# The last down projection with 16 of its 44 weight chunks as seven block products

## The reference

```
f = rms_norm_2(h, ffn_norm_g)
h = h + (silu(f @ ffn_w1) * (f @ ffn_w3)) @ ffn_w2        # ffn_w2: 5632 x 2048
h = h + (p @ pl_w_up) * sigmoid(h @ pl_w_gate)            # pl_w_gate: 2048 x 2048
return rms_norm_2(h, final_norm_g)
```

## Time and profile before

| | us |
|---|---|
| median of 3 runs | 2418.42 (2418.24 to 2418.65) |
| profiled execution: span from the first to the last instruction | 2417.2 |
| profiled execution: its own time | the profile gives the span alone; the median is 1.2 above it |
| TensorE busy in it | 2404.8 (99%), 10956 matmuls |
| VectorE busy | 1389.7 (57%) |
| ScalarE busy | 1170.4 (48%) |
| GpSimd busy | 127.4 (5%) |
| DMA queue of SP, share of 16 engines | 68.0% |

### The profile page before, as it was taken

The page is one execution under the profiler, slowest core; times in us unless marked ns, Lnnn a source line. Parts: engine busy times, 40 slices in busy tenths (PEclk is TensorE's granted clock), DMA queues, the critical chain, the costliest instruction groups (busy, mean ns, idle before and its releaser), DMA issues.

```text
span 2417.2 us, 27743 instructions
## 1 busy us (share of the span) xinstructions
PE 2404.8 (99%) x10956; PEld 2000.9 (83%) x10956; DVE 1389.7 (57%) x1192; ACT 1170.4 (48%) x1110; POOL 127.4 (5%) x138
## 2 busy tenths in 40 slices
PE   9999999999999999999999999999999999999998
PEld 8888888888888888888888888888888888888886
DVE  6877645656666666544666474664545445444446
ACT  5554554656656556333455464454343433433335
POOL 5000000001111011000000000000010100100000
PEclk9999999999999999999999999999999999999999
DMA  7566556587777778755698855776766767666663
GB/s 257 187 205 204 167 179 199 179 301 237 234 243 252 235 235 253 276 205 193 202 299 279 254 174 175 231 245 211 230 211 214 221 208 226 231 225 213 213 229 123
DMA packets 276834, 535.16 MB, mean 221 GB/s; under 512 B 12634, under 2 KB 47376, under 8 KB 275856
## 3 DMA queue, kind: packets, MB, share of 16 engines
q1 hardware_dynamic: 276304, 533.21, 68.0%
q10 hardware_dynamic: 448, 0.79, 0.1%
HBM read 495.15 MB, written 39.59 MB: 221 GB/s over the span
## 4 chain that ended last, share of the span: by engine, by line
PE 99%; ACT 1%; DVE 0%; DMA 0%; issue 0%; DVEq 0%; SPq 0%; ACTq 0%
PE ps L1462 31%; PE ps L1464 31%; PE ps L1463 31%; PE ps L1455 2%; PE ps L1456 1%; PE ps L1700 1%; PE ps L1438 0%; PE ps L1715 0%; DMA h<-in_x_dram 0%; ACT w_hi L819 0%; PE ps L1840 0%; PE ps L1684 0%; PE ps L1721 0%; PE ps L1751 0%; DVE w_lo L1898 0%; ACT g_work L984 0%
## 5 line engine op out<-in xcount | busy, mean ns | idle before, releaser
L1898 DVE TENSOR_TENSOR w_lo<-raw,w_hi 128x2048 fp32r<-128x2048 f32 x424 | 980.5, 2312 | 986.4 <-ACT w_hi L819 986.1
L819 ACT ACTIVATE w_hi<-raw 128x2048 fp32r<-128x2048 f32 x424 | 812.8, 1917 | 1207.7 <-PE ps L1464 1168.5
L1462 PE MATMUL ps<-w_hi,xa 128*128 128x512 f32 x1856 | 723.6, 390 | 0.0
L1464 PE MATMUL ps<-w_hi,xa 128*128 128x512 f32 x1856 | 722.2, 389 | 0.0
L1463 PE MATMUL ps<-w_lo,xa 128*128 128x512 f32 x1856 | 722.1, 389 | 0.0
L1462 PE MATMUL ps<-w_hi,g 128*128 128x512 f32 x1408 | 549.2, 390 | 0.0
L1464 PE MATMUL ps<-w_hi,g 128*128 128x512 f32 x1408 | 547.9, 389 | 0.0
L1463 PE MATMUL ps<-w_lo,g 128*128 128x512 f32 x1408 | 547.8, 389 | 0.0
L1464 PEld LDWEIGHTS ps<-w_hi,xa 128*128 128x128 f32 x1856 | 348.4, 188 | 72.7
L1462 PEld LDWEIGHTS ps<-w_hi,xa 128*128 128x128 f32 x1856 | 348.4, 188 | 72.4 <-DVE w_lo L1905 0.2
L1463 PEld LDWEIGHTS ps<-w_lo,xa 128*128 128x128 f32 x1856 | 348.4, 188 | 71.8
(11 more groups left out here) (315 smaller groups left out, 997.6 us busy)
## 6 DMA issues: line engine op xcount, KB each, us to landing
raw<-in_ffn_w_dram SPq DMA_DIRECT2D x132, 1024.0 KB, 5.2
raw<-in_w_in_dram SPq DMA_DIRECT2D x94, 1024.0 KB, 5.2
raw<-in_w_up_dram SPq DMA_DIRECT2D x88, 1024.0 KB, 5.9
raw<-in_w_down_dram SPq DMA_DIRECT2D x44, 1024.0 KB, 5.4
raw<-in_w_out_dram SPq DMA_DIRECT2D x32, 1024.0 KB, 5.1
raw<-in_w_pg_dram SPq DMA_DIRECT2D x16, 1024.0 KB, 7.2
raw<-in_pl_w_gate_dram SPq DMA_DIRECT2D x16, 1024.0 KB, 6.0
up_turned_rows<-h SPq DMA_DIRECT2D x22, 512.0 KB, 3.0
```

What stands on the lines that cost most here:

```text
L819: A(w_hi[j % SPLIT][:, :], raw[s][:, :], ACT.Copy).then_inc(sem("w_hi_ready"), 1)
L1462: mm(o, high, hi, start=begin, stop=False)
L1464: return mm(o, low, hi, start=False, stop=end)
L1898: V.tensor_tensor(w_lo[j % SPLIT][:, :], raw[j % RAW][:, :], w_hi[j % SPLIT][:, :].bitcast(F32), ALU.subtract).then_inc(sem("w_lo_ready"), 1)
```

## The change

In each of `down2` and `down2b` a chunk now holds two k-tiles of 128 rows and all 1024 columns, not four k-tiles and 512 columns; all four banks are filled from chunk 0 to chunk 21. For the 28 ordinary chunks `eight_products` issues 24 matmuls, first those of banks 0 and 1, then those of banks 2 and 3. For chunks 3, 5, ... 17 of each stage `seven_products` issues 21: the 2x2 block product (two token halves, two k-tiles, two column halves) is done with seven block products, not eight. That takes sums of weight blocks and sums of activation blocks.

The weight sums: GpSimd makes the first two (`early_sums`), VectorE the third in place in `raw` and the fourth (`late_sums`); `high` of that chunk waits for the third; ScalarE rounds the three sums that are not in `raw` (`sums_high`), VectorE takes their low parts (`low_sums`). The activation sums ("forms"): during `glu` GpSimd makes four of 128x128 for each of eight iterations (`form_sums`, `form_lows`), ScalarE rounds them, SP stores them in DRAM, and in `down2` and `down2b` SP reads them back, 512 KB for each of the 16 chunks (`take_forms`, behind the load of the chunk two later). The products go to banks 4 to 7 as well; VectorE merges them after chunk 17.

The quads of `h` are turned elsewhere: quads 0 and 1 at positions 3 and 7 of `down2b` (SP's transfers at 8, 9, 12 and 13), quads 2 and 3 at position 21 of it (SP's transfers in `pg2`). The return of the 2 MB embedding and the gain row moves from `down2` and the start of `pg2` to the second iteration of `pg2`. Some semaphores of earlier stages are merged, with the same waits.

```diff
+SEVEN = {"down2": (3, 5, 7, 9, 11, 13, 15, 17), "down2b": (3, 5, 7, 9, 11, 13, 15, 17)}
+SEVEN_BEFORE = {"down2": 0, "down2b": 8}
+FORM_TILES = range(1, 9)
...
+            def paired(ph, w, c0, at):
+
+                for j in range(plan[ph]["body"]):
+                    if j in at:
+                        at[j]()
+                    load(ph, 0, j, weight(w, 2 * j, 2, c0, 1024))
+                    if j - 2 in SEVEN[ph]:
+                        take_forms(ph, j - 2)
+
+            def put_forms(e):
+
+                first = (e - 1) * 1024
+                sp.wait_ge(sem("forms_low"), e)
+                sp.dma_start(forms_dram[:, first:first + 1024] if isinstance(e, int) else forms_dram[:, bass.ds(first, 1024)],
+                             forms[:, :].bitcast(F32)).then_inc(sem("forms_stored"), 16)
+
+            def take_forms(ph, c):
+
+                n, first = SEVEN[ph].index(c), (c // 2 - 1) * 1024
+                sp.wait_ge(sem("forms_stored"), 16 * (c // 2))
+                sp.wait_ge(sem("chunks_multiplied"), chunk_no(ph, 0, c - 4) + 1 if n >= 2 else plan[ph]["chunk"])
+                sp.dma_start(form_factors[ph][n % 2].bitcast(F32), forms_dram[:, first:first + 1024]).then_inc(sem(f"forms_landed{n % 2}"), 16)
...
-                if ph == "pg1":
+                if ph == "pg1" or (ph, q) == ("pg2", 3):
...
+            def glu_fifth(i):
+
+                if isinstance(i, int) and i == 0:
+                    take_h_blocks("glu", 2)
+                elif not isinstance(i, int) or i >= 3:
+                    put_forms(i - 2)
+
+            columns("glu", [(t["ffn_w1_2"][0], 0), (t["ffn_w3_2"][0], 0)], 512, peel=3,
+                    at={4: at_step(0, lambda: put_h_blocks("glu", 2)), 5: glu_fifth,
                         6: lambda i: put_h_blocks("glu", 3) if isinstance(i, int) and i == 0 else put_blocks(i),
                         7: lambda i: take_h_blocks("glu", 3) if isinstance(i, int) and i == 0 else take_blocks(i)})
             w = t["ffn_w2_2"][0]
-            columns("down2", [(w, 0), (w, 512)], 1024, kts=FT,
-                    at={6: lambda i: put_blocks(plan["glu"]["iters"]), 7: lambda i: take_blocks(plan["glu"]["iters"]),
-                        8: take_second,
-                        16: lambda i: put_h_blocks("pg2", 0), 17: lambda i: take_h_blocks("pg2", 0)})
-            columns("down2b", [(w, 1024), (w, 1536)], 1024, kts=FT,
-                    at={5: lambda i: put_h_blocks("pg2", 1), 6: lambda i: take_h_blocks("pg2", 1),
-                        16: lambda i: put_h_blocks("pg2", 2), 17: lambda i: take_h_blocks("pg2", 2)})
+            paired("down2", w, 0,
+                   at={6: lambda: put_blocks(plan["glu"]["iters"]), 7: lambda: take_blocks(plan["glu"]["iters"])})
+            paired("down2b", w, 1024,
+                   at={8: lambda: put_h_blocks("pg2", 0), 9: lambda: take_h_blocks("pg2", 0),
+                       12: lambda: put_h_blocks("pg2", 1), 13: lambda: take_h_blocks("pg2", 1)})
             columns("pg2", [(t["pl_w_gate_2"][0], 0), (t["pl_w_gate_2"][0], 512)], 1024, peel=2,
-                    at={5: at_step(0, lambda: put_h_blocks("pg2", 3)),
-                        6: both(at_step(0, lambda: take_h_blocks("pg2", 3)), load_final_row)})
+                    at={0: at_step(1, lambda: take_h_blocks("pg2", 3)), 2: at_step(1, take_second),
+                        6: at_step(0, lambda: put_h_blocks("pg2", 2)),
+                        7: at_step(0, lambda: (take_h_blocks("pg2", 2), put_h_blocks("pg2", 3))), 5: at_step(1, lambda: load_final_row(0))})
...
+            def form_sums(e):
+
+                if not (isinstance(e, int) and e == FORM_TILES[0]):
+                    pool.wait_ge(sem("forms_stored"), (e - 1) * 16)
+                of = lambda k, a: staged_tile(staged, k)[:, a]
+                s1, s2, s3, s4 = [forms_work[:, 512 + P * n:512 + P * (n + 1)].rearrange("p (i r) -> p i r", r=32) for n in range(4)]
+                pool.tensor_tensor(s3, of(2, 0), of(2, 1), ALU.subtract)
+                pool.tensor_tensor(s1, of(2, 1), of(3, 1), ALU.add).then_inc(sem("forms_summed"), 1)
+                pool.wait_ge(sem("forms_summed"), e * 3 - 2)
+                pool.tensor_tensor(s2, s1, of(2, 0), ALU.subtract).then_inc(sem("forms_summed"), 1)
+                pool.wait_ge(sem("forms_summed"), e * 3 - 1)
+                pool.tensor_tensor(s4, of(3, 0), s2, ALU.subtract).then_inc(sem("forms_summed"), 1)
+
+            def form_lows(e):
+
+                pool.wait_ge(sem("forms_high"), e)
+                pool.tensor_tensor(forms[:, 512:1024], forms_work[:, 512:1024], forms[:, 0:512].bitcast(F32), ALU.subtract)\
+                    .then_inc(sem("forms_low"), 1)
+
             def glu_lows(i):
+                formed = not isinstance(i, int) or i in FORM_TILES
+                if isinstance(i, int) and i == plan["glu"]["iters"] - 1:
+                    early_sums("down2", SEVEN["down2"][0])
                 pool.wait_ge(sem("glu_high"), i + 1)
+                if formed:
+                    form_sums(i)
                 for a in range(2):
                     last = pool.tensor_tensor(in_blocks(g[:, bass.ds(i * 4, 4), S + a * P:S + (a + 1) * P]), staged_half(staged, a),
                                               in_blocks(g[:, bass.ds(i * 4, 4), a * P:(a + 1) * P].bitcast(F32)), ALU.subtract)
                 last.then_inc(sem("glu_low"), 1)
+                if formed:
+                    form_lows(i)
+
+            def early_sums(ph, c):
+
+                no = seven_no(ph, c)
+                pool.wait_ge(sem(f"raw_landed{c % RAW}"), landed_count(ph, c))
+                n = SEVEN[ph].index(c)
+                pool.wait_ge(sem("chunks_multiplied"), chunk_no(ph, 0, c - 4) + 1 if n >= 2 else plan[ph]["chunk"])
+                blocks = raw[c % RAW][:, :].rearrange("p (k b n) -> p b k n", k=2, b=2)
+                pool.tensor_tensor(sums[no % 2][:, 0:1024].rearrange("p (k n) -> p k n", k=2), blocks[:, 1],
+                                raw[c % RAW][:, 0:1024].rearrange("p (k n) -> p k n", k=2), ALU.subtract).then_inc(sem("early_sums"), 1)
...
-            iterations(pool, "glu", glu_lows)
+            iterations(pool, "glu", glu_lows, peel=2, tail=2)
+            for ph in SEVEN:
+                for c in SEVEN[ph][ph == "down2":]:
+                    early_sums(ph, c)
...
+                seven = ph in SEVEN and i == 0 and j in SEVEN[ph]
+                if seven:
+                    act.wait_ge(sem("sums"), 2 * seven_no(ph, j) + 1)
                 A(w_hi[j % SPLIT][:, :], raw[s][:, :], ACT.Copy).then_inc(sem("w_hi_ready"), 1)
+                if seven:
+                    act.wait_ge(sem("sums"), 2 * seven_no(ph, j) + 2)
+                    A(sums_high[ph], sums[seven_no(ph, j) % 2], ACT.Copy).then_inc(sem("sums_high"), 1)
...
+                SEVEN["down2"][-1]: lambda i: copy_first_product("down2")})
             stream("down2b", unroll=True, at={
-                3: lambda i: staged_high("pg2", 1),
-                14: lambda i: staged_high("pg2", 2)})
+                6: lambda i: staged_high("pg2", 0),
+                10: lambda i: staged_high("pg2", 1),
...
+                1: steps({0: lambda: staged_high("pg2", 2)}),
...
+            def three(b, high, low, hi, lo, begin, end):
+
+                mm(bank(b), high, hi, start=begin, stop=False)
+                mm(bank(b), high, lo, start=False, stop=False)
+                return mm(bank(b), low, hi, start=False, stop=end)
+
+            def eight_products(ph, j, hi, lo):
+
+                for gr in range(2):
+                    if j == 0:
+                        group_free(ph, 0, gr)
+                    for a in range(2):
+                        for k in range(2):
+                            x = g[:, 2 * j + k, :]
+                            c = slice((2 * k + gr) * 512, (2 * k + gr + 1) * 512)
+                            last = three(2 * gr + a, x[:, a * P:(a + 1) * P], x[:, S + a * P:S + (a + 1) * P], hi[:, c], lo[:, c],
+                                         j == 0 and k == 0, j == plan[ph]["body"] - 1 and k == 1)
+                        if j == plan[ph]["body"] - 1 and gr != a:
+                            last.then_inc(sem("half_multiplied"), 1)
+                return last
+
+            def seven_products(ph, j, hi, lo):
+
+                no, n = seven_no(ph, j), SEVEN[ph].index(j)
+                begin, end = n == 0, j == SEVEN[ph][-1]
+                slot_ = form_factors[ph][n % 2]
+                early, late = g[:, 2 * j, :], g[:, 2 * j + 1, :]
+                block_ = lambda w, b: w[:, 512 * b:512 * (b + 1)]
+                form = lambda m: (slot_[:, P * m:P * (m + 1)], slot_[:, 512 + P * m:512 + P * (m + 1)])
+                if begin and no:
+                    pe.wait_ge(sem("products_read"), 1)
+                three(4, early[:, 0:P], early[:, S:S + P], block_(hi, 0), block_(lo, 0), begin, end)
```

(90 more changed lines are left out.)

161 lines of the change are left out of this document (94 added, 67 removed).

## The result

| us | before | after |
|---|---|---|
| median (range) | 2418.33 (2417.97 to 2418.65), 4 runs | 2448.98 (2445.93 to 2450.93), 4 runs |
| profiled execution: its time / its span | span 2417.2 | 2445.93 / 2444.2 |
| last matmul starts | 2407.61 | 2434.59 |
| TensorE busy, matmuls | 2404.8, 10956 | 2405.0, 10908 |

The account below looks back on a forecast made before the run. The prediction took TensorE, 99% of the chain, to bound the kernel. Seven terms added 35.4 us and removed matmuls took 10.9 off: +24.5 on the span of 2417.2, 2441.7, with 1.2 for the median 2443 us, range 2427 to 2454.

Parts of the forecast that it names:

- (c): Rival: the clock falls in all four long waits, costing 12 in place of 4.1, plus longer waits: 2453 us; chance 0.13.
- step 3: `down2b`, chunks 7 and 11: forms land late, queued behind the turned quads' store and reads; 4.7 us each, 9.5 together.
- step 4: `pg2` (start P), chunks 2 and 4: turn of quad 3 and reads of quad 2 hold up weights; 2.7 and 2.9, 5.6 us.
- step 7: Granted clock falls in three long waits, and matmuls run at half rate for a while afterwards; 4.1 us (0 to 12).
- step 6: `glu`: GpSimd's activation sums make its second low meet a `w_lo` in eight iterations; 1.0 us (0 to 2.5).
- step 1: `down2`, chunk 0: banks 2 and 3 are wanted while the gate product stands behind `w_lo` of chunk 1; 3.6 us.
- step 2: `down2`, chunk 5: GpSimd's weight sum stands behind `glu_lows`, and its next sum blocks VectorE's third; 6.5 us.
- step 5: Pairs in `down2`, `down2b`: GpSimd's sums block VectorE, late loads, second turn and `add_pair` add delays; 5.1 us (1.5 to 8).
- (b): Rival: GpSimd and VectorE do not block each other for these operand shapes; 2431 us; chance 0.12.
- (a): Rival: the slack holds, TensorE stays busy and 10.9 go; faster, 2407.5 or up to 2412 us; chance 0.05.

Follow-up runs that it names:

- e12: e9 with the last block product of each of the 16 chunks of 21 issued twice, so 24 matmuls in every chunk: 2422.58 us.
- e9: Against the kernel after: gate product first, nothing on GpSimd in `down2` and `down2b`, quads, last low half and `glu_high` moved behind urgent work: 2411.93 us.
- e1: Kernel after, but in the last `glu` iteration VectorE does the gate product before `w_lo` of chunk 1 of `down2`: 2443.26 us.
- e2: Kernel after, but GpSimd makes the weight sum of chunk 5 of `down2` before the last `glu_lows`: 2441.34 us.
- e7: Kernel after, but GpSimd's sum of chunk 7 of `down2` waits until VectorE has made the third sum of chunk 5: 2448.87 us.
- e10: Kernel after, but VectorE makes `early_sums` in front of `w_lo` of the chunk before, not GpSimd: 2435.71 us.
- e3: Kernel after, but in `down2b` SP issues the forms of chunks 7 and 11 ahead of the store of the turned quad: 2445.76 us.
- e4: Kernel after, but quad 3 has its own buffer and DRAM rows, and SP reads quad 2 right behind its store: 2440.44 us.
- e11: e9 with the first two weight sums of each chunk of 21 back on GpSimd, 16 instructions: 2416.15 us.
- e5: Kernel after with all long waits repaired at once: gate product first, GpSimd sums before the last low halves, quad transfers moved, quad 3 buffered separately: 2423.66 us.
- e8: Kernel after, but in `down2b` SP stores turned quads at 9 and 13 and reads them at 11 and 15: 2444.11 us.
- e6: e5 with the last block product of each of the 16 chunks of 21 issued twice, 24 matmuls again: 2429.45 us.

## Why the prediction was right, and where it was not

The direction and the range held; the forecast was 6.0 below the median and 2.9 below the profiled execution. The median lies nearer to rival (c), 2453. That the sum is as near as it is owes something to luck: step 3 was 2.1 too high, steps 4, 7 and 6 were 1.7, 1.7 and 0.9 too low. Its steps against the trace after (excess over 0.227 between starts, in that stretch):

| step | forecast | measured |
|---|---|---|
| matmuls removed | -10.9 | -10.9 (48 fewer, at 0.227; e12 against e9: 10.65) |
| 1 banks at chunk 0 | 3.6 | 3.5 |
| 2 sum behind `glu_lows` | 6.5 | 6.4 |
| 3 forms behind turned quads | 9.5 | 4.17 + 3.23 = 7.4 |
| 4 quads 2 and 3 | 5.6 (2.7 + 2.9) | 4.78 + 2.51 = 7.3 |
| 5 port and order in the pairs | 5.1 | 5.3 |
| 6 `glu` | 1.0 | 1.9 |
| 7 clock | 4.1 | 2.6 + 1.6 + 1.6 = 5.8 |
| sum, last matmul against before | 24.5 | 27.0 (0.3 of it ahead of `glu`) |

**Steps 1 and 2** were right in place, mechanism and size. e1 and e2 show the order on VectorE and on GpSimd as the cause, e7 and e10 the port. That GpSimd's next sum would go ahead of the waiting VectorE was a choice in the prediction (6.5, against 4.2 if not). It came out so, and e7, which takes the choice away, gives back 1.4 of the 2.3: the sum of chunk 7 then meets `w_lo`, at 3.03.

**Step 3** was right in its chain: the forms did wait behind the reads. It was 2.1 too high because chunk 11 came with 3.23 and chunk 7 with 4.17, not 4.7 each; in e1, e2 and e7 chunk 11 has 4.1. The reading "the forms are late" was too narrow, though, as e3 shows: the loads behind the same reads are late as well, and as soon as the forms no longer cover it, they hold TensorE. That the time was the same, 3.6, was chance: about half of it is GpSimd's sum beside `staged_low`. Step 5's "chunks 9 and 13 ... 1.3 each" has this with the wrong size.

**Step 4, chunk 2, is the term that failed in size,** 4.78 in place of 2.7. The prediction took 3.0 to landing for the store, and 2.8 more if a load is ahead. From an issue at P+5.75 that is P+11.6 and not the 10.3 that stands there without a working; with 11.6 its own steps give a wait of about 4.0. So most of the miss is in the sum. The rest is that the store took 6.62: of the five loads that had gone out in the 12 us ahead of it two had not landed when it was issued, and it landed 1.25 after the last of them. e4 confirms the wait itself: with it gone its fall of the clock goes too.

**Steps 5 and 6** come near in their sums, but not by the parts that were forecast. In step 5 chunks 9 and 13 of `down2b` wait 0 and 0.8, not 1.3 each, and small delays of the pairs make it up: 1.6 in `down2` where 0.6 was taken. In step 6 the small delays of eight iterations come to 0.8. One wait of 1.05 in iteration 6, which was not forecast, is the greater part: ScalarE stands 4.32 at `glu_high` until the last of four reads has landed, 7.6 after its issue, with a `w_hi` behind it. In the other variants, with the same work of GpSimd there, `glu` takes 0.7 to 2.1 more than before.

**Step 7** bounded the price of a fall well (1.6 or 2.6, against 0 to 4.8), but had too few falls. Of the six waits of over 2 us in the profiled execution after, three had one; of the 41 such waits in the profiles of this kernel and all its variants, 33. The other executions of the kernel after have a granted clock of 0.992 to 0.994 against 0.996 in the profiled one, and are 2.6 to 5.0 longer. Worked out from the mean clock (an estimate), the low level stood for some 25 to 35 us of them ahead of the last matmul, against 13.7 in the profiled one. So the 3 us between that execution and the median are in all likelihood more falls; no trace of these executions exists to count them.

**Rivals.** (b), no blocking, is refuted by e7, e10 and e11. (c), a fall in every long wait, is what e5, e7 and e8 show for their waits of over 2 us; four falls cost 8.4 in e8 and five 11.9 in e7, where (c) has 12 for four. (a), the slack holds, is false for this kernel but not in itself: in e9 the `w_lo` behind each of the 16 chunks of 21 ends 0.25 to 0.36 ahead of the matmul that wants it, which with the 0.14 of the earlier trace rows is a slack of 0.11 to 0.22, as small as the forecast's 0.12, and it loses only 2.1 of the 10.9 in `down2` and `down2b`. (0.7 more is in the first 300 matmuls of the program, 0.9 in `glu` and ahead of it, 0.2 in `pg2`: 7.0 are left, which is what the two profiled executions are apart. The medians are 6.5 apart: the profiled execution of the kernel before, with its span of 2417.2, is longer than those on record beside e9, 2416.5 to 2417.0.) The slack was not too small; what stood ahead of the urgent work in each queue was too much. The prediction did not say that.

The Trainium skill, "SBUF — State Buffer" (Summary: rules for kernel authors), says that when VectorE has two inputs in SBUF and GpSimd reads SBUF, the second of them to issue stands until the first is done, and advises to schedule whichever is off the critical path. The traces agree: in e11 a `w_lo` that starts 1.29 into a sum of 2.41 takes 3.27 and not 2.29. They also show that the advice can't be followed by busy shares: GpSimd was busy for 9% of the kernel after, and its 16 sums still cost 4.2 us (e11 against e9).

## What to carry to other kernels

Before TensorE is given less work, go through each engine's queue and ask what stands ahead of the preparation of the next chunk: a DMA's landing, a store, another engine's result. Such a wait costs TensorE whatever the slack doesn't cover, and one repaired alone can hand its time on to the next place (e1, e3, e8; not e4). Work given to GpSimd is not free for VectorE: the same sum was 1.22 us in an idle place of VectorE and up to 2.4 us of blocking from GpSimd. The full price of a matmul comes only with the last wait gone: of 10.9, e5 gained less than nothing, e9 6.5.

How long VectorE's `w_lo` takes is the quickest sign of a busy port. Added up over `down2` and `down2b`, what it takes above 2.29 is 5.9 us in the kernel after, 9.5 in e5, 9.1 in e11 and nothing in e9 and e10.

## What was not expected of the hardware

- The granted clock fell to 0.5 in or just after waits as short as 2.13 (e6), 2.42 and 2.88 us (e5), and did not in others of 3.23 and 3.53 (kernel after) and 3.63 (e3). The same wait of 3.53 at chunk 0 had a fall in e2, e3, e7 and e8 and none in the kernel after and e4. After a wait the low level cost 1.3 to 1.7 or 2.3 to 2.9 us of matmuls.
- With both engines ready, GpSimd's next instruction took the port ahead of VectorE, which had been waiting (2.84 in the kernel after and 2.81 in e1, against 0.69 in e7).
- The stretch before the clock first stands at 1.00 differs between the profiled executions, 5.4 us from the start of the span in e5 and 10.4 in e9; the first 300 matmuls took 52.4 and 53.8. A us of difference between two profiled executions can come from there. Whether it goes with the program or with the execution is open, with one trace of each.
